# Gate table of a retrieval FFN: built by adding scatters into a zeroed DRAM table instead of one-hot matmuls

## The reference, cut to what matters

```
s = einsum('thpd,pkd->thpk', q, peer_subkeys)          # two halves, 128 sub-keys each
sv, si = top_k(s, 16)
cand = sv[:,:,0,:,None] + sv[:,:,1,None,:]             # 256 candidates of a head
cidx = si[:,:,0,:,None] * 128 + si[:,:,1,None,:]
fv, fi = top_k(cand, 16)
eidx = take_along_axis(cidx, fi)
gate = softmax(fv)
act  = gelu(einsum('thkd,td->thk', peer_u[eidx], x))
out  = einsum('thk,thkd->td', gate * act, peer_v[eidx])
h    = layer_norm(ALPHA * h + out)
```

## Time and profile before

| | us |
|---|---|
| median of 3 runs | 4359.24 (4354.56 to 4363.43) |
| profiled execution, its own time | 4361.14 |
| its span in the trace | 4359.4 |
| columns 32 to 55 and the transposes before them | about 2171 to 2510 |
| plain columns after them | 2510 to 3244 |
| value blocks | 3244 to 4302 |

### The profile page before, as it was taken

The page is one execution under the profiler, slowest core; times in us unless marked ns, Lnnn a source line. Parts: engine busy times, 40 slices in busy tenths (PEclk is TensorE's granted clock), DMA queues, the critical chain, the costliest instruction groups (busy, mean ns, idle before and its releaser), DMA issues.

```text
span 4359.4 us, 70474 instructions
## 1 busy us (share of the span) xinstructions
PE 4170.0 (96%) x26539; PEld 4004.9 (92%) x26539; DVE 2535.9 (58%) x4045; ACT 1345.8 (31%) x1865; POOL 717.2 (16%) x513
## 2 busy tenths in 40 slices
PE   8998979989899989999999999999999999999996
PEld 6788979989587979999999999999999999999996
DVE  3323233341212355666477746666679888998986
ACT  3432211231212132232355522222223333333333
POOL 0000010020000020024200011111123333344430
PEclk9989989989968999999999999999999999999998
DMA  6532222223431212233334489999999999999993
GB/s 225 203 99 64 73 65 78 69 65 117 167 142 49 73 54 77 79 115 123 124 127 166 169 304 354 355 351 355 356 325 399 410 401 403 392 399 398 400 392 134
DMA packets 495259, 943.14 MB, mean 216 GB/s; under 512 B 126340, under 2 KB 375872, under 8 KB 443000
## 3 DMA queue, kind: packets, MB, share of 16 engines
q1 hardware_dynamic: 443520, 567.36, 39.0%
q0 software_dynamic: 51616, 374.19, 21.4%
HBM read 866.63 MB, written 73.56 MB: 216 GB/s over the span
## 4 chain that ended last, share of the span: by engine, by line
PE 92%; DVE 3%; DMA 2%; ACT 2%; DVEq 1%; issue 0%; POOL 0%; SPq 0%; ACTq 0%
PE pl L1072 24%; PE pp L196 24%; PE pp L1131 12%; PE pt L1131 6%; PE pl L1131 6%; PE pp L1040 5%; PE pt L1049 2%; PE pp L775 2%; PE pp L991 2%; PE pp L956 1%; PE pp L975 1%; PE pt L775 1%; PE pp L842 1%; PE pl L775 1%; PE pt L948 1%; PE pl L1003 1%
## 5 line engine op out<-in xcount | busy, mean ns | idle before, releaser
L1072 PE MATMUL pl<-h_hi,ut_hi 128*128 128x384 f32 x2048 | 734.7, 359 | 0.6 <-ACT ijt L1384 0.6
L1072 PE MATMUL pl<-h_hi,ut_lo 128*128 128x384 f32 x2048 | 692.3, 338 | 0.0
L1072 PE MATMUL pl<-h_lo,ut_hi 128*128 128x384 f32 x2048 | 691.3, 338 | 0.0
L1704 DVE TENSOR_TENSOR ut_lo<-pp,ut_hi 128x512 fp32r<-128x512 f32 x508 | 350.2, 690 | 483.4 <-ACT ut_hi L1337 480.8
L1337 ACT ACTIVATE ut_hi<-pp 128x512 fp32r<-128x512 f32 x508 | 304.0, 599 | 822.0 <-PE pp L1040 765.6
L211 DVE TENSOR_TENSOR w_lo<-raw,w_hi 128x2048 fp32r<-128x2048 f32 x120 | 274.7, 2290 | 425.1 <-ACT w_hi L206 425.0
L1409 ACT ACTIVATE v_hi<-v_raw 128x1024 fp32r<-128x1024 f32 x256 | 272.0, 1062 | 686.0 <-PE pl L1131 508.1
L1072 PEld LDWEIGHTS pl<-h_lo,ut_hi 128*128 128x128 f32 x2048 | 387.1, 189 | 0.0
L1072 PEld LDWEIGHTS pl<-h_hi,ut_hi 128*128 128x128 f32 x2048 | 386.2, 189 | 0.8 <-ACT ijt L1384 0.8
L1806 DVE TENSOR_TENSOR v_lo<-v_raw,v_hi 128x1024 fp32r<-128x1024 f32 x256 | 313.7, 1226 | 124.9 <-ACT v_hi L1409 121.8
L1072 PEld LDWEIGHTS pl<-h_hi,ut_lo 128*128 128x128 f32 x2048 | 384.7, 188 | 0.0
(11 more groups left out here) (359 smaller groups left out, 8262.8 us busy)
## 6 DMA issues: line engine op xcount, KB each, us to landing
u_raw<-in_peer_u SPq DMA_DIRECT2D x256, 512.0 KB
v_raw<-in_peer_v SPq DMA_DIRECT2D x256, 512.0 KB
p_f<-p_scr SPq DMA_DIRECT2D x256, 192.0 KB
raw<-in_w_in SPq DMA_DIRECT2D x24, 1024.0 KB, 5.6
g_scr<-gs POOLq DMA_DIRECT2D x6, 4096.0 KB, 13.7
raw<-in_w_mk SPq DMA_DIRECT2D x16, 1024.0 KB, 4.9
raw<-in_w_mv SPq DMA_DIRECT2D x16, 1024.0 KB, 4.8
raw<-in_w_out SPq DMA_DIRECT2D x16, 1024.0 KB, 5.8
```

The source lines that it names most:

```text
L1072: last = mm(pl[:, d, 0:N], w[:, d, k, :], x[:, k, S:S + N], start=(k == 0 and w is ut_hi and x is h_hi), stop=(k == KC - 1 and w is ut_lo))
L1704: tt(ut_lo[:, d, 4 * g:4 * g + 4, :], src.rearrange("p (c i) -> p c i", c=4), ut_hi[:, d, 4 * g:4 * g + 4, :].bitcast(F32), ALU.subtract). ...
```

## The change

The gate table becomes `[128 i, 128 j, 384 tokens]`. While the query projection of the attention runs on PE (16 panels), POOL writes zeros to it with 16 DMAs of 1.5 MB, one behind each panel. The softmax is made head by head: DVE subtracts the maximum in `pick`, ACT takes the exponent in its column loop at row 26 + 12*h (`gate_exp`), and DVE normalises and computes for each of 3 x 16 values of the head a list of 128 cell numbers (`gates_of`). POOL then adds the gates to the table with indirect DMAs: each takes one column of `gix` (128 cell numbers) and one of `gz` (128 values of 4 bytes), 48 a head, 384 in all. At each head's first it waits until all adds of the heads before have landed. 14 (IN_HEAD) are issued in each of the last 6 turns of the candidate loop, and 14 in front of each gather from the eighth on, until none is left. The transposes of indices and gates, the one-hot matrices, their matmuls, their copies and the six stores are gone. Gathers begin right behind the selection. STEP_COL goes from 62 to 36: DVE makes one step in each of columns 36 to 61 and 1.5 in a column from there, so 26 more than before at the same column. AHEAD goes from 60 to 62, where SP now waits for all 384 adds. The loads of gate rows are whole rows of 1536 bytes.

```diff
-AHEAD = 60
-STEP_COL = 62
+AHEAD = 62
+STEP_COL = 36
...
-        g_scr = nc.dram_tensor("g_scr", [2 * ND, P, NK, HALF], F32).ap()
+        g_scr = nc.dram_tensor("g_scr", [NK, P, N], F32).ap()
+        g_cells = g_scr.rearrange("i j t -> (i j t)").rearrange("(c x) -> c x", x=1)
...
+        SCATTERS = [(h, t, k) for h in range(PH) for t in range(ND) for k in range(h * TOPK, (h + 1) * TOPK)]
+        IN_HEAD = 14
...
@@ SP, column AHEAD @@
-                    for s in range(2):
-                        sp.wait_ge(g_stored[s], 16 * ND)
+                    sp.wait_ge(g_added, 16 * len(SCATTERS))
...
@@ PE, column @@
-                        if gate is not None:
-                            gate_matrix(group(gate, k // 4)[0], k // 4 % 2)
...
@@ ACT, column @@
+                    if isinstance(i, int):
+                        row = 4 * (2 * i + d + 1) + g
+                        for h in range(PH):
+                            if row == exp_row(h):
+                                gate_exp(h)
...
@@ DVE @@
+            def gates_of(h):
+                dve.wait_ge(g_exp, h + 1)
+                gz_h = gz[:, :, h * TOPK:(h + 1) * TOPK]
+                nc.vector.tensor_reduce(sums[:, 0, 0:NT1], gz_h, AX.X, ALU.add)
+                dve.wait_ge(pool_step, PICK_STEPS * (h + 1))
+                ij_h = ij[:, :, 1:1 + ND, h * TOPK:(h + 1) * TOPK]
+                stt(pair[:, :, :], ij_h[:, 0], float(NK), ij_h[:, 1], ALU.mult, ALU.add)
+                dve.drain()
+                nc.vector.reciprocal(sums[:, 1, 0:NT1], sums[:, 0, 0:NT1])
+                stt(gix[:, :, h * TOPK:(h + 1) * TOPK], pair[:, :, :], float(N),
+                    tok[:, :].rearrange("p (t k) -> p t k", k=1).to_broadcast([P, ND, TOPK]), ALU.mult, ALU.add)
+                dve.drain()
+                tt(gz_h, gz_h, sums[:, 1, 0:NT1].rearrange("p (t k) -> p t k", k=1).to_broadcast([P, NT1, TOPK]), ALU.mult)\
+                    .then_inc(gates_ready, 1)
...
             for h in range(PH):
                 pick(h)
+                if h >= 1:
+                    gates_of(h - 1)
...
+            for b in range(PICK, AHEAD):
+                for g in range(4):
+                    rows_lo((b + 1) // 2, (b + 1) % 2, g, turn_bank(g))
+                    if g == 3 and b >= STEP_COL:
+                        step()
             for b in range(AHEAD, NK):
-                upto = max(0, b + 1 - STEP_COL) * 3 // 2
+                upto = AHEAD - STEP_COL + (b + 1 - AHEAD) * 3 // 2
...
@@ POOL @@
+            g.memset(zero[:, :], 0.0).then_inc(zero_ready, 1)
+            pool.wait_ge(zero_ready, 1)
+            for n in range(16):
+                pool.wait_ge(panel_done, MQ0 + n)
+                pool.dma_start(g_scr[8 * n:8 * n + 8].rearrange("b p t -> p b t"),
+                               zero[:, :].rearrange("p (b t) -> p b t", b=1).to_broadcast([P, 8, N])).then_inc(g_zeroed, 16)
+            pool.wait_ge(g_zeroed, 16 * 16)
...
+            def scatter(count):
+
+                for h, t, k in SCATTERS[scattered[0]:scattered[0] + count]:
+                    if t == 0 and k == h * TOPK:
+                        pool.wait_ge(gates_ready, h + 1)
+                        if h >= 1:
+                            pool.wait_ge(g_added, 16 * ND * TOPK * h)
+                    g.indirect_dma_start(g_cells, bass.IndirectOffsetOnAxis(gix[:, t, k:k + 1], 0), gz[:, t + 1, k:k + 1], None,
+                                         compute_op=ALU.add).then_inc(g_added, 16)
+                scattered[0] += count
...
             for h in range(PH):
...
+                if h >= 2:
+                    scatter(IN_HEAD)
...
-            for ht in range(2 * ND):
-                pool.wait_ge(g_out, 16 * (ht + 1))
-                pool.dma_start(g_scr[ht], gs[:, ht % 2]).then_inc(g_stored[ht % 2], 16)
-            for s in range(2):
-                pool.wait_ge(g_stored[s], 16 * ND)
             pool.wait_ge(smp_in, 16 * 11)
             for n in range(NSTEP):
                 if n >= NG_BUF:
+                    if scattered[0] < len(SCATTERS):
+                        scatter(min(14, len(SCATTERS) - scattered[0]))
                     pool.wait_ge(step_done, n - NG_BUF + 1)
```

More of the change, by code:

```diff
@@ L536, in program, with exp_row @@
         NSTEP = 2 * (NS + P)
-        def gate_columns(eng, column):
-            for ht in range(2 * ND):
[L542 to L555, removed]
+        SCATTERS = [(h, t, k) for h in range(PH) for t in range(ND) for k in range(h * TOPK, (h + 1) * TOPK)]
+        IN_HEAD = 14
+        def exp_row(h):
+            return 26 + 12 * h
         @block.sync
@@ L1041, in turn_rows @@
                 last.then_inc(t_done, 1)
[L1043 to L1050, removed]
             def sparse_rows(x):
@@ L1062, in sparse_rows, with column @@
                 last.then_inc(xr_done, 1)
-            def column(i, d, gate=None, more=True):
+            def column(i, d, more=True):
                 if not (isinstance(i, int) and i == 0):
@@ L1093, in _ @@
                     column(i, d)
[L1094 to L1106, removed]
-            pe.wait_ge(ijt_out, 3)
-            gate_columns(pe, column)
-            with pe.Fori(PICK // 2 + 4 * ND, NK // 2 - 1) as i:
+            with pe.Fori(5, NK // 2 - 1) as i:
                 for d in range(2):
@@ L1343, in gelu, with gate_exp, column @@
                 f(fg[:, d, :], pl[:, d, 0:N], ACT.Gelu_apprx_tanh).then_inc(ge_done, 1)
-            def column(i, d, gate=None, more=True):
+            def gate_exp(h):
+                act.wait_ge(g_sub, h + 1)
+                gz_h = gz[:, :, h * TOPK:(h + 1) * TOPK]
+                f(gz_h, gz_h, ACT.Exp).then_inc(g_exp, 1)
+            def column(i, d, more=True):
                 first = isinstance(i, int) and i == 0 and d == 0
@@ L1371, in _ @@
                     scores_out(15)
-            for i in range(5):
+            for i in range(PICK // 2):
                 for d in range(2):
                     column(i, d)
-            with act.Fori(5, PICK // 2 - 1) as i:
-                for d in range(2):
-                    column(i, d)
-            act.wait_ge(g_sub, 1)
-            f(gw[:, :, :], gw[:, :, :], ACT.Exp).then_inc(g_exp, 1)
-            for d in range(2):
-                column(PICK // 2 - 1, d)
-            for x in range(3):
-                act.wait_ge(ijt_done, x + 1)
-                f(ijt[:, x, :], pt[0][:, 0:N], ACT.Copy).then_inc(ijt_out, 1)
-            gate_columns(act, column)
-            with act.Fori(PICK // 2 + 4 * ND, GELU_S) as i:
+            with act.Fori(PICK // 2, GELU_S) as i:
                 for d in range(2):
@@ L1729, in _ @@
[L1729 to L1734 removed]
             while turned[0] < 4 * (PICK + 1):
                 next_rows(1)
[L1737 removed]
+            gates_of(PH - 1)
             dve.wait_ge(xr_done, 8)
@@ L1748, in one_hot @@
-            def one_hot(n, s, t0):
-                if not (isinstance(n, int) and n < 2):
-                    dve.wait_ge(g_done, n - 1)
-                for x in range(4):
-                    ts(oh[:, s, 0, x, :], iota_k[:, :], ijt[:, 1, bass.ds(t0 + x, 1)], None, ALU.is_equal)
-                    last = ts(oh[:, s, 1, x, :], iota_k[:, :], ijt[:, 0, bass.ds(t0 + x, 1)],
-                              ijt[:, 2, bass.ds(t0 + x, 1)], ALU.is_equal, ALU.mult)
-                last.then_inc(oh_ready, 1)
@@ L1757, in gate_column @@
-            def gate_column(i, d, gate):
-                for g in range(4):
-                    n, t0 = group(gate, g)
-                    one_hot(n, g % 2, t0 + HALF * gate[0])
-                    rows_lo(i + d, 1 - d, g, turn_bank(g))
-            gate_columns(dve, gate_column)
             done = [0]
```

66 lines of the change are left out of this document (23 added, 43 removed).

## The result

| | us |
|---|---|
| before, median of 4 runs beside the changed kernel | 4359.7 (4354.6 to 4363.4) |
| changed kernel, median of 4 runs | 4650.0 (4649.7 to 4653.9) |
| ratio | 1.067, 95% interval 1.065 to 1.069 |
| forecast | 4435, range 4252 to 4515 |

The change made the kernel slower by 290 us. The sign was forecast, the size was not: the time lies 215 us above the forecast and outside its range.

The account below looks back on a forecast made before the run. The prediction took PE, busy for 96% of the span, as the bound. Stall 165 + selection 8 - one-hot work 92.7 - value blocks 5 gave +75 us on a span of 4359.4: 4435 us, range 4252 to 4515.

Parts of the forecast that it names:

- The price of a scatter: POOL's time per adding indirect DMA, start to start, taken from the gather's spacing: 1.25 us.
- The upper bound of the prediction: Highest price of a scatter: a gather just behind a two-SBUF-input DVE instruction, 1.91 us, with 0.30 between two: 2.2 us.
- c: Symbol for the price of one scatter on POOL, taken as 1.25 us; each 0.1 us moves the result 28.6 us.
- The stall: Behind the selection, DVE and PE wait for gathers queued behind 14 scatters each on POOL: 165 us.
- The selection: Six turns with 14 scatters each make POOL's turn longer than PE's 30.56 us: +8 us (0 to 15).
- Softmax by head: Five small DVE instructions and two ACT table loads a head: 0, at worst 1 us a head.
- One-hot work: PE saves the one-hot products of 24 columns, 88.1 us, and the transposes with their copies, 4.6: -92.7 us.
- Value blocks: 26 of 320 steps leave the value blocks for earlier columns, so PE is short less: -5 us (0 to 8).
- Zeroing: 16 DMAs of 1.5 MB behind the panels, hidden in POOL's idle time: 0, at worst 10 us.
- B: Rival: a scatter costs POOL only a direct DMA's 0.50 us, no stall: 4262 us; chance 0.34 with its neighbours.
- C: Rival: adds are slow in the DMA engines, 3.1 us each without overlap: 4888 us; chance 0.08 including half of it.
- Its halfway case: Half of C's 3.1 us for each scatter in the DMA engines: 4521 us; counted within C's chance of 0.08.

Follow-up runs that it names:

- e1: Changed kernel with the 384 scatters as plain copies in place of adds; 4574.2 us, ratio 1.049.
- e5: Changed kernel with the 384 adding scatters replaced by plain gathers of 4-byte cells into a spare tile; 4606.6 us, ratio 1.058.
- e2: Changed kernel with no scatters and no wait for them, dense gates left out; 4275.7 us, ratio 0.981.
- e6: e2 with the eight calls that finish a head's gates moved behind the selection's loop; 4257.6 us, ratio 0.977.
- e7: e2 with a head's gates finished earlier, behind the wait for POOL's index sums and ahead of the comparison releasing the next; 4257.8 us, ratio 0.977.
- e11: Changed kernel with only the 84 scatters inside the selection, and a head's gates finished where e7 has them; 4308.3 us, ratio 0.987.
- e3: Changed kernel with every second scatter left out, 7 in a turn and 7 before a gather; 4369.5 us, ratio 1.002.

## Why the prediction was wrong, step by step

- **The price of a scatter, 1.25 us: this is the step that failed.** It measured 1.85 (1.541 + 0.30; e1 gives 0.57 of it to the add). With 286 scatters on the path and 14 in each of six turns, that one term makes nearly the whole miss of 215 us. "The data of 4 bytes instead of 8 KB changes nothing that POOL does by number" was right, a plain copy took 0.967 us; that the add is itself work of POOL was not considered. The upper bound of the prediction, 2.2 us, held it, but the forecast's own range ended at c = 1.5. (The low bound called 0.50 is 0.51 to 0.52 in the earlier trace rows; hardly anything hangs on it.)
- **The stall, 165 us: the mechanism held, the size follows from c.** By the prediction's own relation 165 + 286 x 0.595 = 335 us; measured 340.5. The batch: 14 x 1.845 + 1.3 = 27.1 us and one delay, measured 28.2. Its signs were all there: DVE's steps waited 376 us for gathers, PE for `ut_lo`, and the last wait was SP's at column 62 (released at 2868). That the sum closes so well has some luck in it: the relation holds for adds, but at a price of 1.27 us it fell short by far (e1, e5), for the prediction has no term for PE held at its issue. With a cheap copy in place of the add, the forecast would have missed too.
- **The selection, +8 us: +55.5.** c was too small again, and 1.2 us of the turn were not counted: 2.4 + 11.7 + 14 x 1.85 + 1.2 = 41 us, measured 40.9. Six turns of 10.3 us over are 62, of which the columns show 55.5.
- **Softmax by head, 0: wrong, and covered.** By itself its place costs 24 us (e2 against e6 and e7); in the changed kernel POOL's longer turn hides them (e11). I had counted five small instructions by their size and not asked what POOL does when they come, though the earlier trace rows were used for just such a pair with the roles turned round.
- **One-hot work, -92.7 us: -96.4.** The forecast read one pair of gelus, 13.86 us; columns 33 to 55 lasted 13.94 on average, and column 32, with the transposes, 20.32 us, 6.4 more than these, where 4.6 were counted.
- **Value blocks, -5 us: -7.0** for value blocks and tail, inside the bounds.
- **Zeroing, 0: right.** POOL did wait for the last zeros, and the memset of the earlier trace rows came 3 us earlier than before all the same:

```profile
1076.91 0.89 POOL L1919 DMA_DIRECT2D g_scr<-zero  x1 [11.83 <-PE pp L197]
1088.66 3.94 POOL L1923 MEMSET qm<- 128x4608 f32 x1 [10.86 <-DMA g_scr<-zero]
```

- **Rivals.** B (a cheap scatter) is out: even without the add POOL needs 0.967 us. C (slow in the DMA engines) is out: POOL waits for adds to land for only 19 us in all, at the heads' borders, and half the adds cost far less than half the stall (e3). Its halfway case gave 4521 for a price of 1.55 us; POOL's own price went past that.

In terms of the sum: 4435 + 176 (stall) + 47 (selection) - 4 (one-hot work) - 2 (value blocks) - 3.5 (start, no more than what varies) = 4648.5; the span was 4648.4.

## What to carry to other kernels

An operation that the trace does not show is bounded by its nearest row, but each attribute in which it differs from that row (here the add) wants a bound of its own, and the range must reach it when the result is multiplied by some 300 instances. Work that goes to an idle engine is free only up to that engine's room beside the bound one: write the room down in the operation's own units (30.56 us a turn less 15.3 leave 8 scatters, not 14), and give it exactly that much; a third of this change came out 31 us under the kernel before, where the whole lost 290. Before a small instruction with two SBUF inputs is put beside GpSimd's work, look which long GpSimd instruction is released just ahead of it.

## What the runs showed of the hardware

- An indirect DMA of 128 cells of 4 bytes holds GpSimd 0.967 us as a plain scatter (e1), 0.955 as a plain gather (e5), and 1.541 us as an adding scatter; 0.30 us lie between two. An 8 KB-row gather takes 0.94. An adding scatter makes 112 packets more than a plain one (111936 against 68928 for 384).
- A DVE instruction on 48 elements with two SBUF inputs lasted 5.45 us beside a GpSimd tensor_tensor and 0.17 us away from it.
- Plain 4-byte indirect DMAs back to back, one every 1.26 us, went with TensorE starting an instruction only every 2.8 us, with no semaphore to wait for. At 3 us a DMA (one run, with a memset and a drain between), or with adds at 1.85, this was not seen.
- TensorE's granted clock fell to 0.70 and 0.53 in the stalled stretches and was back at 0.99 in the window that begins at 2880 us.
